# Six jobs instead of four in the phase that loads the first modulation of a two-block transformer kernel

## The reference

```python
def first_block(x, c, positions, w_ada, b_ada, norm_mix, norm_ffn, w_in, ...):
    c_act = jax.nn.silu(c)
    mod = c_act @ w_ada[l] + b_ada[l]                     # (1, 6 * 2048)
    sh_a, sc_a, gt_a, sh_f, sc_f, gt_f = split(mod, 6)
    h = _rmsnorm(x, norm_mix[l]) * (1.0 + sc_a) + sh_a
    p = h @ w_in[l]                                       # (256, 9296)
    c_q, c_kv, k_pe, q_g, k_g, v_g, z, b_logit, a_logit, gate_logits = _split_cols(p)
    y_a = _mla_branch(c_q, c_kv, k_pe, ...) @ w_o_mla[l]
    y_b = _gdn_branch(concat([q_g, k_g, v_g]), z, b_logit, a_logit, ...) @ w_o_gdn[l]
    g_a, g_b = split(sigmoid(gate_logits), 2)
    x = x + gt_a * ((g_a * y_a + g_b * y_b) @ w_o[l])
    ...                                                   # FFN with sh_f, sc_f, gt_f
```

## Time and profile before

| | us |
|---|---|
| median of 3 runs | 2295.18 (2292.54 to 2296.31) |
| the profiled execution | 2293.58, of which the span is 2292.3 |
| TensorE busy | 2235.2 (98%) |
| VectorE busy | 1505.7 (66%) |
| ScalarE busy | 1009.0 (44%) |
| HBM read | 502.51 MB |

### The profile page before, as it was taken

One profiled execution on the slowest core, in us unless ns is written; L12 is line 12 of the kernel. 1 busy time (PEld: TensorE's weight loads), 2 busy tenths in 40 slices (PEclk: granted clock), 3 DMA queues, 4 the chain that ended last, 5 costly groups with the idle time before them and its releaser, 6 DMA issues.

```text
span 2292.3 us, 26935 instructions
## 1 busy us (share of the span) xinstructions
PE 2235.2 (98%) x10767; PEld 1855.7 (81%) x10767; DVE 1505.7 (66%) x1927; ACT 1009.0 (44%) x1270; POOL 24.4 (1%) x28
## 2 busy tenths in 40 slices
PE   5998999999999999999999999999999999999998
...
GB/s 363 381 240 209 245 228 258 198 271 197 220 269 307 275 239 285 273 242 202 184 192 193 184 202 184 191 195 193 191 195 188 188 188 190 187 185 194 197 189 130
DMA packets 276445, 506.75 MB, mean 221 GB/s; under 512 B 24032, under 2 KB 38112, under 8 KB 275296
## 3 DMA queue, kind: packets, MB, share of 16 engines
...
HBM read 502.51 MB, written 2.49 MB: 220 GB/s over the span
## 4 chain that ended last, share of the span: by engine, by line
PE 82%; DVE 8%; DMA 4%; ACT 2%; issue 2%; SPq 0%; POOL 0%; DVEq 0%; ACTq 0%
PE bank L1200 25%; PE bank L1202 25%; PE bank L1201 25%; DVE WL L1927 3%; PE bank L1391 2%; DMA RAW<-in_w_o_dram 2%; DVE GA L1908 1%; PE bank L1121 1%; ACT WH L1480 1%; PE bank L1212 1%; PE bank L1214 1%; PE bank L1213 1%; DMA RAW<-in_w_o_gdn_dram 1%; PE bank L1148 1%; PE bank L1363 1%
## 5 line engine op out<-in xcount | busy, mean ns | idle before, releaser
L1927 DVE TENSOR_TENSOR WL<-RAW,WH 128x1024 fp32r<-128x1024 f32 (+1 forms) x714 | 864.9, 1218 | 619.2 <-ACT WH L1480 616.5
L1480 ACT CAST WH<-RAW 128x1024 fp32r<-128x1024 f32 (+1 forms) x714 | 743.3, 1047 | 917.6 <-PE bank L1202 733.1
L1200 PE MATMUL bank<-WH,HTh 128*128 128x512 f32 x1936 | 770.4, 398 | 7.3 <-DVE WL L1927 6.5
L1202 PE MATMUL bank<-WH,HTl 128*128 128x512 f32 x1936 | 755.9, 390 | 0.0
L1201 PE MATMUL bank<-WL,HTh 128*128 128x512 f32 x1936 | 755.5, 390 | 0.0
L1200 PEld LDWEIGHTS bank<-WH,HTh 128*128 128x128 f32 x1936 | 364.2, 188 | 88.7 <-DVE WL L1927 11.3
L1201 PEld LDWEIGHTS bank<-WL,HTh 128*128 128x128 f32 x1936 | 364.4, 188 | 77.1 <-issue 4.3
L1202 PEld LDWEIGHTS bank<-WH,HTl 128*128 128x128 f32 x1936 | 364.0, 188 | 76.5
L1908 DVE SCALAR_TENSOR_TENSOR GA<-RAW,ST,GA 128x512 f32<-128x512 f32 x264 | 181.2, 747 | 13.9 <-DMA RAW<-in_w_ada_dram 7.7
L1200 PE MATMUL bank<-WH,R2h 128*128 128x512 f32 x408 | 164.1, 402 | 3.5 <-DVE WL L1927 3.5
L1202 PE MATMUL bank<-WH,R2l 128*128 128x512 f32 x408 | 159.9, 392 | 0.0
...
## 6 DMA issues: line engine op xcount, KB each, us to landing
...
```

Source lines behind the costliest of these rows:

```text
L1200: e.matmul(o, ah[:, s], hi[:, k, :], start=first, stop=False)
L1202: i = e.matmul(o, al[:, s], hi[:, k, :], start=False, stop=last)
L1480: e.copy(hi, rv).then_inc(S["hi"], 1)
L1927: e.tensor_tensor(lo, rv, hi.bitcast(F32), ALU.subtract).then_inc(S["lo"], 1)
```

## The change

- `front` has six jobs: sm, conv 0 (q0), cq, conv 1 (q1), ckv, ga 0, in this order in each round. conv 0, conv 1 and ga 0 all use banks 6 and 7, and close their sum after each round's four k-tiles; a new step `acc` copies the sum to SBUF (`CS`) in round 0 (ScalarE) and adds it there in rounds 1 to 3 (VectorE, two 128x512 additions each).
- The second chunk of a round stands on TensorE between the two halves of ga 0. `mod_e` and `h` of the next round are written behind `acc` of ga 0 and the splits of sm.
- In round 3 the steps of cq's norm, and the rope tables, are written between the jobs' halves, the rope tables ahead of ckv's halves and ga 0's splits.
- The first eight chunks are computed in columns: for each of four blocks of 128 columns, two matmuls of one column over `GA` and four over the fourth load, with c as the moving side. `mod_e` is then two 128x4 additions. `CB` and `JX` are gone.
- conv 0 and conv 1 are evicted from SBUF by `first_convs`, ga 0 with ga 1.
- The later chunks' loads: `thick` is now ga 3, gb 1 to 3 and og 0 to 3; none in conv 2 and in the up projections. `gate_row` has six slots, not four, before its matmul.

```diff
...
@@ -107,8 +109,10 @@
              Job("ckv", 1, plain(win, O_CKV), 16, 512, "ht", lazy=True),
-             conv(0, O_Q)]
-    a1 = [conv(1, O_Q + 512), conv(2, O_K)]
+             conv(0, O_Q), conv(1, O_Q + 512), Job("ga", 0, plain(win, O_GATE), 16, 512, "ht")]
+    for n in range(3):
+        front[3 + n].acc = n
+    a1 = [conv(2, O_K)]
     a1 += [Job("uqn", c, heads(a["w_uq"], 192, 4 * c, 4, 0, P), 4, 512, "lat0", side="ch", own=c == 1) for c in range(2)]
@@ -116,7 +120,8 @@
     for c in range(4):
-        b1.append(Job("ga", c, plain(win, O_GATE + 512 * c), 16, 512, "ht"))
+        if c < 3:
+            b1.append(Job("ga", c + 1, plain(win, O_GATE + 512 * (c + 1)), 16, 512, "ht"))
         b1.append(Job("om", c, rowpart(a["w_o_mla"], 0, 512 * c), 8, 512, "omla"))
@@ -231,9 +236,8 @@
         self.XT0 = by_head(64, 4096)
-        self.CB = ar(57, 512).rearrange("p (t n) -> p t n", n=P)
-        self.JX = ar(97, 512).rearrange("p (j n) -> p j n", n=P)
         self.tmp1 = [ar(32, 1024), ar(36, 1024)]
+        self.CS = [ar(16, 1024), ar(20, 1024), ar(96, 1024)]
         self.qT, self.kT = by_head(24, 2048), by_head(32, 2048)
...
@@ -356,16 +360,17 @@
             f = [("g", 2 * c + 2 + i // 4, i % 4) for i in range(8)] if c < 3 else []
-            w = [("w", j, 4 * c, 4) for j in jobs[:4]]
-            u.extend([w[0]] + f[:1] + [w[1]] + f[1:5] + [w[2]] + f[5:] + [w[3]])
+            sm, cq, ckv, q0, q1, ga = (("w", j, 4 * c, 4) for j in jobs[:6])
+            u.extend([sm] + f[:1] + [q0] + f[1:2] + [cq] + f[2:3] + [q1] + f[3:5] + [ckv] + f[5:6] + [ga] + f[6:])
         self.start_units = len(u)
-        order = [(j, t0) for j in jobs[4:] for t0 in range(0, j.nkt, j.step)]
+        order = [(j, t0) for j in jobs[6:] for t0 in range(0, j.nkt, j.step)]
         p = [i for i, (j, _) in enumerate(order) if j.name == "wout" and j.c in ((3, 0), (3, 1))]
         order[p[1]], order[p[2]] = order[p[2]], order[p[1]]
-        thick = (("conv", 3), ("conv", 4), ("og", 2), ("og", 3))
+        thick = [("ga", 3), ("gb", 1), ("gb", 2), ("gb", 3)] + [("og", c) for c in range(4)]
+        thin = [("conv", 2)] + [(n, c) for n in ("uqn", "uqp", "ukk", "ukv") for c in range(2)]
         for k, (j, t0) in enumerate(order):
             u.append(("w", j, t0, min(j.step, j.nkt - t0)))
-            never = (("ga", 2), ("gb", 3)) if extra and extra[0][1] < 20 else (("wo", 3), ("gate", 0))
+            never = thin if extra and extra[0][1] < 20 else (("wo", 3), ("gate", 0))
             if extra and (k % 2 or (j.name, j.c) in thick) and (j.name, j.c) not in never:
...
@@ -480,24 +485,51 @@
             self.front_unit()
-            for j in (jobs[0], jobs[1]):
-                self.front_halves(j, where[j.name])
-            for _ in range(4 * more):
+            self.front_half(sm, 2)
+            self.front_half(sm, 2)
+            if more:
                 self.front_unit()
             self.front_unit()
-            self.front_halves(jobs[2], where[jobs[2].name])
+            self.front_half(q0, 3)
+            self.front_half(q0, 3)
             if more:
                 self.front_unit()
+            self.put("acc", 0, c, self.used)
+            self.front_unit()
+            self.front_half(cq, 0)
+            self.front_half(cq, 0)
+            if more:
                 self.front_unit()
+            else:
+                latent = self.done(cq, 0)
+                next(latent)
+            self.front_half(q1, 3)
+            if more:
+                self.front_unit()
+            else:
+                next(latent)
+            self.front_half(q1, 3)
+            self.front_unit()
+            self.put("acc", 1, c, self.used)
+            if more:
                 self.put("mod_e", 2 * c + 2, None)
                 self.put("cam", c + 1)
                 self.front_unit()
+            else:
+                next(latent, None)
+                self.put("rope_tables")
+            self.front_half(ckv, 1)
+            self.front_half(ckv, 1)
             self.front_unit()
             if more:
                 self.front_unit()
-            else:
-                self.put("rope_tables")
-            self.front_halves(jobs[3], where[jobs[3].name])
+            self.front_half(ga, 3)
+            if more:
+                self.front_unit()
+            self.front_half(ga, 3)
+            self.put("acc", 2, c, self.used)
+            if more:
+                self.front_unit()
         self.have |= {("mod", ci) for ci in range(8)} | {("ht", kt) for kt in range(16)}
...
@@ -701,6 +733,8 @@
             self.settle("attention")
+            if c == 1:
+                self.put("ga", 0, None)
             self.put("ga", c, pr)
@@ -778,6 +812,15 @@

+    def first_convs(self):
+        for n in range(2):
+            for i in range(2):
+                self.put("conv", n, i, None)
+                yield
+            self.bg.append(self.conv_rest(n))
+            yield
+            yield
+
     def conv_rest(self, n):
@@ -885,7 +928,7 @@
         name = "gta" if ci < 20 else "gtf"
-        for n in range(4):
+        for n in range(6):
             if n == 2:
@@ -978,9 +1021,8 @@
         self.bg.append(self.attention())
-        self.retire(J["front"][1], 0)
         self.retire(J["front"][2], 1)
-        self.bg.append(self.done(J["front"][3], 3))
+        self.bg.append(self.first_convs())
         self.bg.append(self.done(J["front"][0], 2))
@@ -1040,7 +1082,12 @@

-RAW1_FREE = (("lo", 32), ("mod_t", 8))
+RAW1_FREE = (("lo", 48), ("mod_t", 8))
+
+
+def acc_event(n, c):
+
+    return ("acc_d", 2 * (3 * (c - 1) + n) + 2) if c else ("acc_a", 2 * n + 2)

@@ -1140,12 +1187,16 @@
                 held[n] = [("mod", mod_value(ci))]
-                for h in range(2):
-                    e.matmul(b, ones, L.GA[:, ci % 2, h, :], start=h == 0, stop=False)
-                W.wait_ge("cact", 3)
+                for m in range(4):
+                    for h in range(2):
+                        e.matmul(b[:, m:m + 1], L.GA[:, ci % 2, h, m * P:(m + 1) * P], ones[:, 0:1],
+                                 start=h == 0, stop=h == 1)
+                W.wait_ge("cact", 2)
                 W.wait_ge(f"raw{sch.raw_slot(i)}", sch.raw_value[i])
-                for t in range(4):
-                    i = e.matmul(b, L.CB[:, t, :], rv[:, t, :], start=False, stop=t == 3)
+                for m in range(4):
+                    for t in range(4):
+                        i = e.matmul(b[:, 4 + m:5 + m], rv[:, t, m * P:(m + 1) * P], L.cact[:, 12 + t:13 + t],
+                                     start=t == 0, stop=t == 3)
             else:
@@ -1186,12 +1237,13 @@
                 b, pr = (bank[2 * where], bank[2 * where + 1]), (where,)
-            if t0 == 0 and tiles[0] == 0:
+            group = j.nkt if j.acc is None else 4
+            if t0 % group == 0 and tiles[0] == 0:
                 for n in pr:
                     take(n)
             for k in range(nk):
                 kt = t0 + k
-                first, last = kt == 0, kt == j.nkt - 1
+                first, last = kt % group == 0, kt % group == group - 1
                 ah, al = xh[:, x0 + kt, :], xl[:, x0 + kt, :]
...
@@ -1479,6 +1531,12 @@

+        elif kind == "acc" and args[1] == 0:
+            n, _, done = args
+            W.wait_ge("half", done)
+            for q in range(2):
+                e.copy(L.CS[n][:, 512 * q:512 * q + 512], bank[6 + q]).then_inc(S["acc_a"], 1)
+
         elif kind == "x_rs":
@@ -1596,14 +1654,19 @@
                 W.wait_ge(*RAW1_FREE[1])
-            W.wait_ge("half", job_end(sch, "conv", n))
+            if n < 2:
+                W.wait_ge(*acc_event(n, 3))
+                u = [L.CS[n][:, 512 * q:512 * q + 512] for q in range(2)]
+            else:
+                W.wait_ge("half", job_end(sch, "conv", n))
+                u = [bank[2 * pr], bank[2 * pr + 1]]
             W.wait_ge("nat_t", 2 * n - 2)
             for q in range(2):
                 o = L.CV[n % 2][:, (2 * q + i) * T:(2 * q + i + 1) * T]
                 j = 96 + 24 * 3 + 4 * n + 2 * q + i
                 if i:
                     W.wait_ge("cv_d", 12 * n + 5 + q)
-                e.activation(o, bank[2 * pr + q][:, i * T:(i + 1) * T], ACT.Copy, scale=L.COL[:, j:j + 1]
+                e.activation(o, u[q][:, i * T:(i + 1) * T], ACT.Copy, scale=L.COL[:, j:j + 1]
                              ).then_inc(S["cv_a"], 1)
...
@@ -1926,6 +1992,14 @@

+        elif kind == "acc" and args[1]:
+            n, c, done = args
+            W.wait_ge("half", done)
+            W.wait_ge(*acc_event(n, c - 1))
+            for q in range(2):
+                total = L.CS[n][:, 512 * q:512 * q + 512]
+                e.tensor_tensor(total, bank[6 + q], total, ALU.add).then_inc(S["acc_d"], 1)
+
         elif kind == "x_rs":
@@ -1945,13 +2019,12 @@
             if q is None:
-                b = bank[4 if ci == 1 else 5].rearrange("p (j n) -> p j n", n=P)
-                W.wait_ge("mod", 3 * ci)
```

(11 more changed lines are left out.)

35 lines of the change are left out of this document (22 added, 13 removed).

## The result

The kernel after takes 2374.59 us (median of 4 runs, 2373.16 to 2380.06), the kernel before beside it 2294.52: a ratio of 1.0356, 95% interval 1.0343 to 1.0369. Forecast was 2322, range 2302 to 2336. The sign was right, the size a third of what came.

A forecast was written before the change was run, and what follows sets the result against it. It took the front as bound by its loads, then VectorE from 155.6 to 360.6 us. Front +29, relief -10 and later loads +8 make +27, plus 1.6 to the median, on 2293.6: 2322 us, range 2302 to 2336.

The forecast's parts named there:

- Modulation in columns, 5.4 us a chunk: First eight chunks on TensorE: 5.4 us each against 4.83, so +0.55 a chunk and +4.4 in eight.
- rival B: One-column matmuls hold the clock down behind each of eight chunks, 1.7 to 3 us each: +13 to +24, to 2340; chance 0.12.
- The order inside a round, 49.4 us: Front rounds: 40.0 us of TensorE work plus exposed VectorE chain 4.5, waits 2.1 and 1.3, clock 1.5; bounds 45 and 52.
- The clock: 1.5 us, bounds 0 and 3: In each front round, about 1.5 us of the channel job lost to the lower clock after the hole.
- Start at 42.5: First small job of the front starts at about 42.5 us instead of 43.62.
- Last round 39.0: Front's last round: work 29.3 us plus 1.3, 1.5, 4.3 and 2.6 of idle and clock loss.
- VectorE's relief, -10: Up to conv 5, 6 modulation loads instead of 17 cut TensorE's idle: -10 us, bounds -3 and -16.
- conv 0 and 1 evicted from SBUF: Evictions of both convs: same number and size of instructions on the same engines, so 0, bounds -1 and +2.
- ga 3 +2, gb and og +6: The 11 moved loads cost gate chunk 3 +2 us (0 to 6), gb 3 and og +6 (0 to 14).
- A: New front bound by TensorE's work alone: a round is 40 + 1 us, total time 2285 us; chance 0.08.
- C: Front as forecast but cheaper: rounds at 46 us, VectorE's relief worth 16, total time 2296 to 2305; chance 0.13.
- D: Loads at peak with three buffers stall gb and og by 14 us or more: 2330 to 2335; chance 0.12.

The follow-up runs named there:

- rows_form: Kernel after with the first modulation's chunks formed again in rows, by 512-column matmuls, instead of columns; 2360.29 us, ratio 1.0287.
- before_cols: Kernel before with one edit of the change alone, the first modulation in one-column matmuls; 2323.99 us, ratio 1.0129.
- before_newloads: Kernel before with the change's placement of the later modulation loads alone, less ga 3; 2306.48 us, ratio 1.0052.
- old_loads: Kernel after with the later modulation chunks loaded about where the kernel before has them; 2379.91 us, ratio 1.0369.
- rows_late: Kernel after with the first modulation in rows and ga 0's sum queued behind the next round's mod_e and h; 2350.06 us, ratio 1.0239.

## Why the prediction was wrong

- *Modulation in columns, 5.4 us a chunk.* The failed step. The spacing was read from the earlier trace rows, where the same instruction ran at a clock of 1.00 with much other work of TensorE around it, and was taken to hold in the front. It does hold where the clock does (5.27 us, twice), but most chunks run partly at 1.2 GHz, up to 9.0 us, and what comes behind them too: 20.2 us by rows_form, 29.4 by before_cols. This is rival B, given 0.12 and "1.7 to 3 us" a chunk; measured is 2.5 (20.2 / 8) to 3.7 (29.4 / 8).
- *The order inside a round, 49.4 us.* Right in the main. The chain stands in the trace ahead of rounds 1 to 3 as forecast, with holes of 4.5, 4.3 and 4.3 us (the first small job's is 2.6), and the first big split comes 3.5 us after the small job; of that TensorE waits 0.7 and not 2.1, since the small job ran at 1.2 GHz there. With the columns out of it (rows_form) rounds are 47.8, 50.3 and 51.9. That they come so near 49.4 is partly luck, since the holes there are 5.5 to 5.8 us. "The clock: 1.5 us, bounds 0 and 3" failed: with the columns it is 7.4 to 14.2, and 3.0 to 5.7 even in rows_form. The second chunk's wait of 1.3 should read 1.5 by its own terms (9.7 less 8.2); it is 0.8.
- *Start at 42.5.* 47.7; 43.5 in rows_form. The columns again: chunk 0 takes 10.3 us instead of 7.1, chunk 1 6.4 instead of 5.3. In chunk 0 the records come every 0.21 us, twice the full-clock spacing, though the row of the clock says 1.00 that early. The saving of 1.2 us on VectorE came: the hole is 2.6 us instead of 3.8.
- *Last round 39.0.* 41.0, and 39.3 in rows_form. Right. Its terms ahead of gate chunk 0 add up to 9.3 us, and not 9.7, so 3.9 of idle and not 4.3; the trace shows 4.0.
- *VectorE's relief, -10.* Itself too small: -15.9 (before_newloads), 14.4 by old_loads. But the change took a job of 27 us off TensorE in a stretch that VectorE bounds and left the job's evictions in it, and the prediction put "conv 0 and 1 evicted from SBUF" at 0, bounds -1 and +2. Between the two orders of jobs the stretch differs by 19.7.
- *ga 3 +2, gb and og +6.* +29.6, and +27.1 with the old order of jobs. The upper bounds, 6 and 14, were too low as well. I had costed VectorE's work and the queues' sum of bytes, and not the single wait: in og 1 ScalarE stood 10.9 us for a job's weights, at 346 GB/s (381 in the front before).
- *Rivals.* A (TensorE alone bounds the front) and C did not come: even rows_late's rounds are over 44 us. D named gb and og rightly, at 14 us where that term lost 29.6. No case had B and D together.
